# A windowed attention inside a one-core transformer kernel: values stationary in column halves, division on GpSimd, the sink as a 257th score column

## The chip, the cores and the metric

The kernel runs on one core of one Trainium2 chip. The metric is the device time of one execution in microseconds (us). Three runs of the kernel before took 963.71, 963.83 and 963.84 us; the median is 963.83 us.

## The reference, cut to what matters

The reference runs two blocks over 256 tokens of width 1024 in float32: first a block with an mLSTM layer, a feed-forward layer, a windowed attention and a second feed-forward layer, then a block with two more attentions. The change touches the windowed attention of the first block, called the first attention here:

```python
proj = h @ w_in                                   # 16 query heads, 4 key/value heads of 64
q, k = rope(q, positions), rope(k, positions)
scores = einsum('bcqhgd,bckhd->bchgqk', q, k_band) * (hd ** -0.5)
scores = where(mask, scores, -inf)                # |key - query| <= 128
m = maximum(max(scores, axis=-1), sink_l)
p = exp(scores - m[..., None])
denom = sum(p, axis=-1) + exp(sink_l - m)
out = einsum('bchgqk,bckhd->bcqhgd', p, v_band)
out = out / denom[..., None]
return out.reshape(B, S, Hq * hd) @ w_out         # then added to the residual
```

Each of the 16 query heads has a 256 x 256 score matrix, a sink logit that only enlarges the denominator, and a 256 x 64 output.

## The kernel before

Everything is written out by hand: each engine has one list of instructions (`block.sync`, `block.gpsimd`, the lists of TensorE, ScalarE and VectorE), and semaphores order them. No planner sets an order; what stands earlier in an engine's list runs earlier.

**Products.** Weights come from memory in 56 chunks of 1024 x 512 float32. SyncE loads each as two halves (`main`, L344) when `w_lo_ok` says that the half's old contents were split. ScalarE rounds a half to fp32r (`w_hi`, `split_half`, L1271, recorded at L1273) and VectorE subtracts to get the rest (`w_lo`, `rest_half`, L1806, at L1808). A product is then three matmuls (`mm3`, L450, lines 452 to 454). Activations that become stationary operands are split in the same way into a high and a low half: `to_stationary` (L510, transposes at L523) turns them on TensorE, `split_st` (ScalarE, L1249) writes the high half and counts `st_hi_ok`, `rest_st` (VectorE, L1745) the low half and counts `st_lo_ok`.

**The first attention.** Features of keys and queries lie on the partitions, 32 rows a head and half, so that four heads form a group. Four groups of four heads make the 16 heads, numbered n. The steps of one group j are:

- `a_queries` (L822): the query projection of a group, three matmuls of 256 columns each, 48 for all of it (24 for a half). VectorE rotates the result (`rotated`, L2120, lines 2125 to 2129) and counts `rot_ok`.
- `a_scores` (L837): 16 float32 matmuls, recorded as 32 instructions at L846; head g of the group works on rows 32g to 32g + 31 and writes to its own bank. It waits for `rot_ok` and, from the second group on, until VectorE has read the banks of the group before (`nm_ok`).
- `group_masked` (VectorE, L2186): for each head, two instructions (L2195, one for each half of the queries) scale, add the mask, write the scores `a_sm` to SBUF and take the maximum; after a drain L2199 compares it with the sink and negates it, counting `nm_ok`. After four heads L2202 adds the sinks for the extra term of the denominator.
- `a_exps` (ScalarE, L1494): two exponentials of 256 columns (L1501) with their sums, `p_ok`. It runs three heads ahead of the turns. After each group L1507 takes the exponentials of the sinks.
- `a_turn` (TensorE, L851): four transposes (L857) of the head's unnormalised weights into bank 5. ScalarE copies them to `a_pt` (L1515, two buffers) and counts `pt_ok`.
- `a_values` (TensorE, L861): four float32 matmuls, recorded as 8 instructions at L870. The turned weights are stationary, the 64 value columns move; tokens come out on the rows of bank 7. `o_ps` counts.
- `group_attended` (VectorE, L2205): sums and reciprocals of the group's denominators and one product of 128 x 512 (L2215) that divides the four heads and writes `a_o`, counting `o_ok`.

**The output projection.** `a_o` has tokens on its rows, so each of its 8 column tiles k is turned again: `a_out_turn` (L874), two transposes at L523, then `split_st` and `rest_st` into `y_hi` and `y_lo`. `a_out_tiles` (L881) multiplies tile k with the first half of the output weights: three matmuls of 512 columns for each of two row blocks. `mixer_rest` (L682) does the second half of the columns.

**The order around the change.** TensorE's list (from L887) begins with `a_scores(0)` and `a_queries(2)`. For each group it has: turn of the first head, values of the head before, scores of the next group, half of the last group's queries (j = 0 and 1), then for the three other heads a turn and the values of the head before. All output turns and output tiles stand in and behind the last group. Then come the 8 transposes of the meta tokens (L915), the last two tiles and `mixer_rest`. VectorE's list (from L2220) has, for each j: `group_attended(j - 1)`, `group_masked(j + 1)`, and for j = 0 and 1 a weight half and the rotation of queries 2 + j. ScalarE's list (from L1509) has, for each head n, the copy of turn n, the exponentials of n + 3, and after heads 0, 4 and 7 a weight half (`A_HALVES`, L125). GpSimd has nothing in this stretch: three loads are issued at L436 to L438, three more at L441 to L443 once the attention has been added to the residual (`h_ready` of 3).

## Time and profile before

| | |
|---|---|
| median of three runs | 963.83 us |
| span of the profiled execution | 963.6 us |
| TensorE busy (matmuls) | 939.2 us, 97% |
| VectorE busy | 585.4 us, 61% |
| ScalarE busy | 479.5 us, 50% |
| GpSimd busy | 24.7 us, 3% |
| granted TensorE clock over the span | 0.998 of 2.4 GHz |
| first attention, first scores to second half of its output projection | 348.46 to 405.37 us |

The profile is of one execution, and its span is its own time between the first and the last instruction; it lies 0.2 us below the median of the runs. The engines are named PE (TensorE), DVE (VectorE), ACT (ScalarE), POOL (GpSimd) and SP (SyncE). A TensorE instruction's end is modelled and overlaps its successors, so the distance between two starts says more of the queue than a duration. A float32 matmul appears as two instructions, an fp32r matmul and a transpose as one. Idle time of an engine counts only where another waits for it.

### The profile page before, as it was taken

The numbers are of one execution on the slowest core, as the hardware profiler recorded it, in microseconds if no ns is written. First come the engines' busy times: TensorE is split into PE (matmuls) and PEld (weight loads), VectorE is DVE, ScalarE is ACT, GpSimd is POOL, SyncE is SP. The second block draws the span as 40 slices with busy tenths as digits, with TensorE's granted clock in tenths as the row PEclk, the third lists the DMA queues.
The fourth block names the chain that finished last, engine by engine and source line by source line (L and its number), as shares of the span: only waits on it lengthen the run. The fifth ranks groups of instructions, "written<-read, shape, count | busy, mean of one in ns | idle before, by whom it ended". The sixth has DMA issues, their size and how long they took to land.

```text
span 963.6 us, 13667 instructions
## 1 busy us (share of the span) xinstructions
PE 939.2 (97%) x5035; PEld 779.7 (81%) x5035; DVE 585.4 (61%) x1078; ACT 479.5 (50%) x770; POOL 24.7 (3%) x39
## 2 busy tenths in 40 slices
PE   6999899999999999999999999999999999999996
PEld 6877678888888899878888888889987878878775
DVE  5866857655454678566463644877665556565665
ACT  6565556353443548454443434685344454445442
POOL 0014200000000000000000000000000000000000
PEclk9999999999999999999999999999999999999999
DMA  8542345545546322246546364232423242533441
GB/s 301 211 178 85 103 179 218 209 184 190 201 154 236 134 88 89 88 171 244 194 163 229 131 243 154 85 131 99 165 93 127 88 162 101 175 130 130 166 166 44
DMA packets 25607, 150.30 MB, mean 156 GB/s; under 512 B 3024, under 2 KB 3152, under 8 KB 11344
## 3 DMA queue, kind: packets, MB, share of 16 engines
q1 hardware_dynamic: 24912, 147.44, 41.9%
q0 software_dynamic: 640, 2.11, 0.7%
q8 instruction: 36, 0.59, 0.2%
q14 instruction: 19, 0.16, 0.0%
HBM read 148.50 MB, written 1.05 MB: 155 GB/s over the span
## 4 chain that ended last, share of the span: by engine, by line
PE 84%; DVE 7%; ACT 3%; DMA 3%; DVEq 1%; issue 1%; SPq 0%; ACTq 0%
PE bank L452 24%; PE bank L453 24%; PE bank L454 23%; DMA w_raw<-w_main_dram 3%; DVE w_lo L1808 2%; PE bank L523 1%; PE bank L1009 1%; PE bank L732 1%; DVE arena L2195 1%; PE bank L1024 1%; PE bank L1062 1%; PE bank L870 1%; PE bank L1044 1%; PE bank L1045 1%; PE bank L846 1%
## 5 line engine op out<-in xcount | busy, mean ns | idle before, releaser
L452 PE MATMUL bank<-w_hi,x_hi 128*128 128x512 f32 (+2 forms) x648 | 262.6, 405 | 1.7 <-DVE x_lo L1747 0.9
L453 PE MATMUL bank<-w_lo,x_hi 128*128 128x512 f32 (+2 forms) x648 | 253.9, 392 | 0.0
L454 PE MATMUL bank<-w_hi,x_lo 128*128 128x512 f32 (+2 forms) x648 | 252.2, 389 | 0.0
L452 PEld LDWEIGHTS bank<-w_hi,x_hi 128*128 128x128 f32 x648 | 122.2, 189 | 33.3 <-issue 5.6
L1722 DVE TENSOR_TENSOR w_lo<-w_raw,w_hi 128x2048 fp32r<-128x2048 f32 x50 | 114.4, 2292 | 57.0 <-ACT w_hi L1212 56.5
L454 PEld LDWEIGHTS bank<-w_hi,x_lo 128*128 128x128 f32 x648 | 121.7, 188 | 27.2
L453 PEld LDWEIGHTS bank<-w_lo,x_hi 128*128 128x128 f32 x648 | 122.0, 188 | 22.3
L1212 ACT ACTIVATE w_hi<-w_raw 128x2048 fp32r<-128x2048 f32 x54 | 103.2, 1917 | 58.1 <-DMA w_raw<-w_main_dram 52.0
L1808 DVE TENSOR_TENSOR w_lo<-w_raw,w_hi 128x2048 fp32r<-128x2048 f32 x51 | 116.2, 2283 | 4.8 <-ACT w_hi L1273 4.7
L1273 ACT ACTIVATE w_hi<-w_raw 128x2048 fp32r<-128x2048 f32 x50 | 94.9, 1907 | 14.7 <-DMA w_raw<-w_main_dram 14.2
L452 PE MATMUL bank<-x_hi,w_hi 128*128 128x256 f32 (+1 forms) x272 | 80.4, 296 | 8.9 <-DVE w_lo L1818 8.6
L1414 ACT ACTIVATE ffn_nat<-bank,stat 128x256 f32<-128x256 f32 x44 | 20.9, 474 | 136.9 <-PE bank L454 136.9
L2068 DVE SCALAR_TENSOR_TENSOR ffn_nat<-bank,stat,ffn_nat 128x256 f32<-128x256 f32 x44 | 21.1, 482 | 104.2 <-ACT ffn_nat L1414 104.1
L454 PE MATMUL bank<-x_hi,w_lo 128*128 128x256 f32 (+1 forms) x272 | 77.8, 286 | 0.0
L453 PE MATMUL bank<-x_lo,w_hi 128*128 128x256 f32 (+1 forms) x272 | 77.8, 286 | 0.0
L1490 ACT ACTIVATE arena<-arena,small 128x144 f32<-128x144 f32 x64 | 29.5, 461 | 76.4 <-DVE small L2172 76.4
L452 PE MATMUL bank<-s_hi,g_hi 128*128 128x512 f32 x166 | 65.4, 394 | 0.5 <-ACT arena L1233 0.4
L454 PE MATMUL bank<-s_hi,g_lo 128*128 128x512 f32 x166 | 65.4, 394 | 0.0
L453 PE MATMUL bank<-s_lo,g_hi 128*128 128x512 f32 x166 | 65.3, 393 | 0.0
L452 PEld LDWEIGHTS bank<-x_hi,w_hi 128*128 128x128 f32 x272 | 52.5, 193 | 12.4 <-issue 11.5
L452 PE MATMUL bank<-w_hi,s_hi 128*128 128x512 f32 x128 | 53.1, 415 | 0.7 <-DVE h L1999 0.4
L453 PEld LDWEIGHTS bank<-x_lo,w_hi 128*128 128x128 f32 x272 | 52.6, 193 | 0.0
(357 smaller groups left out, 1452.4 us busy)
## 6 DMA issues: line engine op xcount, KB each, us to landing
w_raw<-w_main_dram SPq DMA_DIRECT2D x111, 1024.0 KB, 4.9
s_raw<-w_side_dram SPq DMA_DIRECT2D x51, 512.0 KB, 4.2
w_raw<-w_main_dram SPq DMA_DIRECT2D x2, 512.0 KB, 6.7
h<-x_dram SPq DMA_DIRECT2D x2, 512.0 KB, 10.9
arena<-rows_dram POOLq DMA_DIRECT2D x2, 512.0 KB, 4.1
arena<-x_t_dram SPq DMA_DIRECT2D x1, 768.0 KB, 7.3
out_dram<-arena SPq DMA_DIRECT2D x1, 512.0 KB, 2.6
out_dram<-arena SPq DMA_DIRECT2D x2, 256.0 KB, 2.1
```

The lines of the kernel that those rows point to most:

```text
L452: pe.matmul(out, ah, bh, start=first, stop=False)
L453: pe.matmul(out, ah, bl, start=False, stop=False)
L454: return pe.matmul(out, al, bh, start=False, stop=last)
L523: ins = pe.transpose(b[:, M + r * P:M + (r + 1) * P], src(r, k), ident[:, :])
L732: ins = pe.transpose(bank[2][:, ks * S + r * P:ks * S + (r + 1) * P], ffn_nat[:, 1, r, ks * P:(ks + 1) * P], ident[:, :])
L1212: act.activation(w_hi[:, slot, 4 * g:4 * g + 4, :], w_raw[:, g, :, :], ACT.Copy).then_inc(w_hi_ok, 1)
L1273: act.activation(w_hi[:, slot, 4 * g:4 * g + 4, :], w_raw[:, g, :, :], ACT.Copy).then_inc(w_hi_ok, 1)
L1414: act.activation(ffn_nat[:, 0, r, :], acc[(n0 + r) % 2][:, 0:256], ACT.Silu, scale=stat[:, 24 + r:25 + r]).then_inc(silu_ok, 1)
L1490: ins = act.activation(tiles(r), tiles(r), ACT.Exp, bias=small[:, s0 + 2 + r:s0 + 3 + r], accum_out=small[:, s0 + 4 + r:s0 + 5 + r])
L1722: dve.tensor_tensor(w_lo[:, slot, 4 * g:4 * g + 4, :], w_raw[:, g, :, :], w_hi[:, slot, 4 * g:4 * g + 4, :], ALU.subtract).then_inc(w_lo_o ...
L1808: dve.tensor_tensor(w_lo[:, slot, 4 * g:4 * g + 4, :], w_raw[:, g, :, :], w_hi[:, slot, 4 * g:4 * g + 4, :], ALU.subtract).then_inc(w_lo_o ...
L2068: dve.scalar_tensor_tensor(out=ffn_nat[:, 1, r, :], in0=acc[b_][:, 256:512], scalar=root_col(r), in1=ffn_nat[:, 0, r, :], op0=ALU.mult, op ...
```

## The change

- The scores `a_sm` have rows of 258 with 257 in use. VectorE copies the sinks into column 256 for a whole group (`sinks`), and the exponentials run over 257 columns, so that their sum is the whole denominator. The extra steps for the sinks (L2202, L1507, `es_in`, `es_ok`) are gone.
- GpSimd takes, for each head, the sum to the power -1 (128 x 2) and multiplies the head's 128 x 2 x 256 weights with it in place; `a_turn` waits for its `pn_ok` instead of `p_ok`.
- `a_values(k)` works on a pair of heads: the 64 value columns are stationary, the turned weights of 256 tokens move, head 2k writes partitions 0 to 63 and head 2k + 1 partitions 64 to 127 of columns 0 to 255 of bank 7. That is already the feature-major tile k which the output projection needs: ScalarE (`a_out_high`) and VectorE (`a_out_low`) split it from there. `group_attended`, `a_o` and `a_out_turn` are gone.
- `a_pt` has four buffers, and the lists of all engines are put in a new order; output tiles stand from the third group on.

```diff
-A_HALVES = {0: (C_AOUT, 0), 4: (C_AOUT, 1), 7: (C_AOUT + 1, 0)}
+A_HALVES = {0: (C_AOUT, 0), 4: (C_AOUT, 1), 7: (C_AOUT + 1, 0), 13: (C_AOUT + 1, 1)}
...
-        a_sm, a_pt = (ar(4224, NG, R, S), ar(9344, NG, R, S)), ar(15744, 2, 4, P)
+        a_sm, a_pt = (ar(4160, NG, R, S + 2), ar(9344, NG, R, S + 2)), ar(6272, 4, 4, P)
...
+            pool.memset(recip, -1.0)
...
+            for n in range(NH):
+
+                st_, g = a_st[:, n // NG % 2, :, :], n % NG
+                t, root = a_sm[n // NG % 2][:, g, :, 0:S], st_[:, 3, g::NG]
+                pool.wait_ge(p_ok, n + 1)
+                pool.tensor_tensor(root, st_[:, 2, g::NG], recip.to_broadcast([P, R]), ALU.pow)
+                pool.drain()
+                pool.tensor_tensor(t, t, root.rearrange("p (r e) -> p r e", e=1).to_broadcast([P, R, S]), ALU.mult).then_inc(pn_ok, 1)
...
-                pe.wait_ge(p_ok, n + 1)
+                pe.wait_ge(pn_ok, n + 1)
...
+            def a_values(k):
+
+                pe.wait_ge(pt_ok, 2 * k + 2)
+                if k == 0:
                     pe.wait_ge(av_ok, 1)
...
+                else:
+                    pe.wait_ge(st_lo_ok, ST["a_out"] + k)
+                for kt in range(2):
+                    for n in (2 * k, 2 * k + 1):
+                        f, g = n % 2 * HD, n % NG
+                        ins = pe.matmul(bank[7][f:f + HD, 0:S], a_v[:, kt, g * HD:(g + 1) * HD],
+                                        a_pt[:, n % 4, 2 * kt:2 * kt + 2, :], start=(kt == 0), stop=(kt == 1))
+                ins.then_inc(tp_ready, 1)
...
                 a_turn(n)
-                if j:
-                    a_values(n - 1)
                 if j < NG - 1:
                     a_scores(j + 1)
+                if j:
+                    a_values(2 * j - 1)
                 if j < 2:
                     a_queries(3, j * KT // 2, (j + 1) * KT // 2)
...
+                else:
+                    a_out_tiles(4 * (j - 2))
+                a_turn(n + 1)
+                if j >= 2:
+                    a_out_tiles(4 * (j - 2) + 1)
+                a_turn(n + 2)
+                a_values(2 * j)
+                if j == 2:
+                    a_out_tiles(2)
+                elif j == 3:
+                    pe.wait_ge(um_ok, 1)
+                    pe.wait_ge(nm_ok, NH)
+                    for k in range(KT):
+                        ins = pe.transpose(bank[6][:, k * M:(k + 1) * M], um[0:M, k * P:(k + 1) * P], ident[0:M, 0:M])
+                    ins.then_inc(um_ps, 1)
+                a_turn(n + 3)
+                if j == 2:
+                    a_out_tiles(3)
             a_out_tiles(KT - 2)
+            a_values(KT - 1)
             a_out_tiles(KT - 1)
...
+            def a_out_high(k):
+
+                act.wait_ge(tp_ready, ST["a_out"] + k + 1)
+                act.activation(y_hi[:, k, :], bank[7][:, 0:S], ACT.Copy).then_inc(st_hi_ok, 1)
...
+                if n >= 4:
+                    act.wait_ge(tp_ready, ST["a_out"] + n // 2 - 1)
+                act.activation(a_pt[:, n % 4, :, :], bank[5][:, :].rearrange("p (a b) -> p a b", a=4), ACT.Copy).then_inc(pt_ok, 1)
                 if n + NG - 1 < NH:
                     a_exps(n + NG - 1)
+                if n >= 2 and n % 2 == 0:
+                    a_out_high(n // 2 - 1)
...
+            def a_out_low(k):
+
+                dve.wait_ge(st_hi_ok, ST["a_out"] + k + 1)
+                dve.tensor_tensor(y_lo[:, k, :], bank[7][:, 0:S], y_hi[:, k, :], ALU.subtract).then_inc(st_lo_ok, 1)
...
             for j in range(NG):
+                n = NG * (j + 1)
+                if j < NG - 1:
+                    sinks(j + 1)
+                    head_masked_a(n)
+                    head_masked_a(n + 1)
                 if j:
-                    group_attended(j - 1)
+                    a_out_low(2 * j - 1)
                 if j < NG - 1:
-                    group_masked(j + 1)
+                    head_masked_a(n + 2)
+                    head_masked_a(n + 3)
                 if j < 2:
                     rest_half(C_AOUT, C_AOUT % 2, j)
                     rotated(("aq", 2 + j), aqT[:, 2 + j, :, :])
...
+                a_out_low(2 * j)
+                if j >= 2:
+                    rest_half(C_AOUT + 1, (C_AOUT + 1) % 2, j - 2)
+            a_out_low(KT - 1)
```

`head_masked_a(n)` is the body of the old loop in `group_masked` for one head.

## Rows read from the trace of the kernel before

**Rows 1.** The page: header and busy time by engine.
```profile
span 963.6 us, 13667 instructions
...
PE 939.2 (97%) x5035; PEld 779.7 (81%) x5035; DVE 585.4 (61%) x1078; ACT 479.5 (50%) x770; POOL 24.7 (3%) x39
```

**Rows 2.** Windows 348.46 to 405.37 us: us, then busy time (instructions) of each engine, clock, DMA.
```profile
348.46:378.56 30.10, 29.54 (x293) 27.43 (x292) 25.34 (x82) 19.66 (x57) 0.00 (x0) 1.00 0.32 114
378.56:405.37 26.81, 26.50 (x196) 22.73 (x196) 15.74 (x45) 15.06 (x42) 0.00 (x0) 1.00 0.29 109
```

**Rows 3.** Timeline of TensorE: start us, us, engine, line, operation, names, shape, count.
```profile
356.13 0.60 PE L857 MATMUL bank<-ident,arena 128*128 128x128 f32 x4
356.93 2.01 PE L846 MATMUL bank<-arena 32*128 32x256 f32 x32 [0.20 <-DVE arena L2199]
...
363.18 0.63 PE L857 MATMUL bank<-ident,arena 128*128 128x128 f32 x4
363.65 1.00 PE L870 MATMUL bank<-arena 128*128 128x64 f32 x8
364.64 0.63 PE L857 MATMUL bank<-ident,arena 128*128 128x128 f32 x4
...
367.71 2.01 PE L846 MATMUL bank<-arena 32*128 32x256 f32 x32
...
378.56 2.01 PE L846 MATMUL bank<-arena 32*128 32x256 f32 x32 [0.24 <-DVE arena L2129]
...
400.94 0.60 PE L523 MATMUL bank<-ident,arena 128*128 128x128 f32 x4
401.47 0.66 PE L915 MATMUL bank<-ident,arena 16*128 16x16 f32 x8
```

**Rows 4.** Timeline of VectorE, 359 to 364 us, same columns.
```profile
359.78 0.23 DVE L2199 TENSOR_SCALAR arena<-arena,par 128x2 f32<-128x2 f32 x1
...
360.77 0.23 DVE L2199 TENSOR_SCALAR arena<-arena,par 128x2 f32<-128x2 f32 x1
...
363.14 2.28 DVE L1808 TENSOR_TENSOR w_lo<-w_raw,w_hi 128x2048 fp32r<-128x2048 f32 x1
```

**Rows 5.** The chain that ended last, in order of time: start us, us, what.
```profile
374.07 2.20 DVEq L2124
...
401.36 0.39 ACT s_hi L1249
401.77 0.44 DVE s_lo L1745
```

**Rows 6.** Timeline of TensorE, 728 to 731 us.
```profile
728.88 1.98 PE L1062 MATMUL bank<-arena 128*128 128x512 f32 x4 [0.33 <-ACT arena L1658]
```

**Rows 7.** Groups of instructions on GpSimd: line, form, count, busy us, mean ns, idle before.
```profile
L428 POOL TENSOR_TENSOR w_lo<-w_raw,w_hi 128x2048 fp32r<-128x2048 f32 x1 | 4.6, 4572 | 6.1 <-DVE w_lo L1808 6.1
L422 POOL TENSOR_TENSOR arena<-arena 128x128 f32<-128x128 f32 x8 | 3.5, 459 | 2.2 <-ACT arena L1347 2.2
```

**Rows 8.** Timelines of GpSimd and VectorE, 79 to 109 us.
```profile
81.55 1.53 POOL L433 TENSOR_SCALAR arena<-arena 128x512 f32<-128x512 f32 x1 [6.06 <-ACT arena L1338]
...
107.01 1.50 POOL L433 TENSOR_SCALAR arena<-arena 128x512 f32<-128x512 f32 x1
...
79.44 2.29 DVE L1808 TENSOR_TENSOR w_lo<-w_raw,w_hi 128x2048 fp32r<-128x2048 f32 x1 [1.79 <-ACT w_hi L1273]
...
107.76 0.17 DVE L1757 TENSOR_SCALAR stat<-stat 128x4 f32<-128x4 f32 x1 [0.98 <-ACT arena L1329]
108.00 0.53 DVE L1761 TENSOR_SCALAR stat<-stat 128x4 int32<-128x4 int32 x1
```

**Rows 9.** Timeline of ScalarE, 353 to 364 us.
```profile
353.87 0.51 ACT L1501 ACTIVATE arena<-arena 128x256 f32<-128x256 f32 x1 [12.12 <-DVE arena L2199]
...
354.77 0.19 ACT L1501 ACTIVATION_READ_ACCUMULATOR arena<-arena 128x1 f32 x1
...
363.92 0.58 ACT L1515 ACTIVATE arena<-bank 128x512 f32<-128x512 f32 x1
```

More of the change, by code:

```diff
@@ L319, in two_blocks @@
         c_bank = (bank[5], bank[7])
-        ang_ok, tab_ok, rot_ok, es_in, es_ok = (sem(n) for n in ("ang_ok", "tab_ok", "rot_ok", "es_in", "es_ok"))
+        ang_ok, tab_ok, rot_ok, pn_ok = (sem(n) for n in ("ang_ok", "tab_ok", "rot_ok", "pn_ok"))
         sc_ps, nm_ok, p_ok, pt_ps, pt_ok, ptm_ok, o_ps, o_ok = (
@@ L2205, in group_attended, with sinks @@
[L2205 to L2218 removed]
+            def sinks(j):
+                if j >= 2:
+                    dve.wait_ge(pt_ps, NG * (j - 1))
+                dve.tensor_copy(a_sm[j % 2][:, :, :, S:S + 1].rearrange("p g r e -> p g (r e)"),
+                                pcol("sink", NG * j, NG).rearrange("p (g r) -> p g r", r=1).to_broadcast([P, NG, R]))
@@ new lines, in head_masked_a @@
+            def head_masked_a(n):
+                j, g = n // NG, n % NG
+                st_ = a_st[:, j % 2, :, :]
+                dve.wait_ge(sc_ps, n + 1)
+                for r in range(R):
+                    dve.tensor_tensor_reduce(a_sm[j % 2][:, g, r, 0:S], as_bank[g][:, r * S:(r + 1) * S], a_mask[:, r, :], HD ** -0.5,
+                                             float(np.finfo(np.float32).min), ALU.add, ALU.max,
+                                             st_[:, 0, r * NG + g:r * NG + g + 1])
+                dve.drain()
+                dve.tensor_scalar(st_[:, 1, g::NG], st_[:, 0, g::NG], pcol("sink", n), -1.0, ALU.max, ALU.mult).then_inc(nm_ok, 1)
@@ L2220, in _ @@
+            def a_out_low(k):
+                dve.wait_ge(st_hi_ok, ST["a_out"] + k + 1)
+                dve.tensor_tensor(y_lo[:, k, :], bank[7][:, 0:S], y_hi[:, k, :], ALU.subtract).then_inc(st_lo_ok, 1)
             dve.wait_ge(c1_landed, 16)
-            group_masked(0)
+            sinks(0)
+            for n in range(NG):
+                head_masked_a(n)
             for j in range(NG):
+                n = NG * (j + 1)
+                if j < NG - 1:
+                    sinks(j + 1)
+                    head_masked_a(n)
+                    head_masked_a(n + 1)
```

97 lines of the change are left out of this document (10 added, 87 removed).

## The prediction

> **What bounds the kernel now.** I read the page first: TensorE is busy for 97% of the span [rows 1], so the first question is what TensorE has to do. Then its timeline around the change, from the first scores of the attention at 348.46 us to the second half of its output projection at 405.37. I cut it at the last of the four score blocks, 378.56, because something else is late on either side. Windows over the two stretches give 30.10 us with 29.54 busy and 26.81 us with 26.50 busy [rows 2]: TensorE hardly waits in either.
>
> In the first stretch it is nevertheless not alone. Score blocks start at 356.93, 367.71 and 378.56 [rows 3], 10.78 and 10.85 us apart. VectorE has a chain of nearly that length between two of them: the scores themselves, 2.01 us [rows 3], four heads at 0.99 each (359.78 to 360.77), then half a weight split and the rotation that the next scores need, from 363.14 to their start at 367.71 [rows 4]: 2.01 + 3.96 + 4.57 = 10.54. The chain that ended last runs over VectorE there [rows 5]. So work taken from TensorE in this stretch buys almost nothing: VectorE's loop is late next. In the second stretch VectorE is busy for 15.74 of 26.81 us and ScalarE for 15.06 [rows 2]; there TensorE's work is the time.
>
> **What the change takes from TensorE.** (a) The eight turns of the attention's output (`a_out_turn`, 16 transposes) go, all of them in the second stretch. Four transposes advance the queue by 0.53 us, 400.94 to 401.47 [rows 3], so eight pairs are 2.1, with the end of a batch in it; I take 1.9. (b) The values: now each head is 8 instructions in 0.99 us, 363.65 to 364.64, and a turn of a head is 0.47, 363.18 to 363.65 [rows 3]. Eight of the sixteen value blocks (heads 8 to 15) lie in the second stretch: 7.9 us. After the change there are eight blocks, one for each pair of heads, with 8 instructions of 256 columns; five of them come behind the last scores. No row has such a column half. From above: four fp32 instructions of 512 columns over the full height take 1.98 us [rows 6], so about 0.46 each with the last one's tail; 256 columns are half, 0.23, and eight one after the other 1.83, with 0.1 for a change of shape 1.92. From below: the scores, four heads on four row groups, put 32 instructions of the same 256 columns into 2.01 us [rows 3], eight in about 0.49; two heads side by side for two key tiles are then 0.97. I add 0.2 for entering and leaving the shape and take 1.17, because two halves that share no output partition are nearest to those row groups. Five blocks are 5.9 us, 2.0 less than now.
>
> The Trainium skill, TensorEngine Tiling (Array Packing), Key Properties, says that tiles load and multiply in parallel, and that a change of the tiling mode drains the engine; with its first half alone the five blocks would be 4.9 us and the kernel 1.0 faster than I forecast. The trace agrees with the first half for the row groups of the scores and shows nothing for column halves.
>
> **What it adds.** (c) GpSimd divides each head before its turn: a power of 128x2, a drain, a product of 128x512. Products of two tensors there cost 0.459 us at 128 columns and 4.572 at 2048 [rows 7], so 2.14 ns a column and 0.18 fixed: 1.28 for 512. From above, its operation of 512 columns with a scalar took 1.50 and 1.53 [rows 8]. I take 1.30, nearest to the line of its own kind. The power appears nowhere: from below it costs the fixed 0.18; from above I allow 2 us, above the whole 512-column operation, since each element may be worked out in software. I take 0.35 with the drain. That makes 1.65 a head, 26 us for sixteen, inside 57. As a throughput it fits; what counts is where a head comes fresh. The first does: its exponentials end at 354.96 [rows 9], VectorE's new copy of the sinks in front adds 0.2 and GpSimd 1.65, so the first turn starts near 356.85 instead of 356.13 and the second scores, right behind it, at 357.35 instead of 356.93: +0.4. Heads 1 to 3 are divided under the scores and queries. Head 4 is fresh again, and so is 8: its exponentials stand behind the copy of head 1 on ScalarE, copy 0.58, exponentials 1.09 [rows 9], GpSimd 1.65, and VectorE's weight split of 2.28 [rows 4] may hold the port before it. That turn waits up to 1.8 us, and all that TensorE has behind it. Its cover is VectorE's rotation, which the scores behind the turn need anyway; some 0.5 us of slack is left. Over 2.0 us a head the cover is gone and each excess is paid.
>
> (d) Turns 1 and 2 now stand with nothing between them, as do 3 and 4: transposes 0.60 [rows 3] and copy 0.58 [rows 9] less 0.47 make 0.8 us of waiting, for each of the first two groups, inside VectorE's loop and free by it. (e) ScalarE's new wait for a pair's values has the next copy and a weight half behind it; the one behind the second scores stands 2 us, while TensorE has 2.9 us of queries. Free. (f) VectorE loses the group divisions, which now lie under TensorE's scores (so nothing), and keeps eight subtractions of 0.44 [rows 5], one of them in the second loop: +0.3. The rotation's last additions read two SBUF tiles and can meet a GpSimd product, 0.3 in each loop; of TensorE's own delay now, 10.8 against 10.54, about as much goes. First stretch in sum: +0.4 + 0.3 - 0.1 = +0.6.
>
> (g) At the end the pair of heads 14 and 15 goes through TensorE, ScalarE 0.39 and VectorE 0.44 [rows 5] before the last output tiles, with nothing between: with 0.2 to fill and drain 1.05 us of waiting. (h) The sink as 257th column is one element per exponential, and four small exponentials go: nothing. (i) The meta-token transposes move, their work does not change. The last weight half is split on VectorE some 2 us later, near 399.8; the load that follows into its buffer is wanted on ScalarE from 407 us on, behind another half, and by TensorE only 11 us later. I cost it at nothing; were it late by those 2 us, ScalarE has room behind it. GpSimd's later loads wait for a point at 418 us, its heads end near 395. SyncE issues in the same order.
>
> **Sum.** Second stretch -1.9 - 2.0 + 1.05 = -2.9 us (rounded), first +0.6, together -2.3. The profiled execution spans 963.6 us [rows 1]; the median is 963.8, so 0.2 lies outside. 963.8 - 2.3 = 961.5 us.
>
> **Rivals.** *Slower, the port shared by VectorE and GpSimd.* The small 128x2 operation that ends each head on VectorE (L2199, `nm_ok`) could be held by a running GpSimd product. For it: the 128x4 operation from SBUF to SBUF at 108.00 took 0.53 us and ended with the GpSimd operation of 107.01. Against it: the like one at 107.76 took 0.17 beside the same operation [rows 8]. Held for 0.5 us at three heads of the first group and 0.9 us in all per loop, the second scores start 1.6 later and two loops are 1.8 longer: 3.4 dearer, 964.9. The sign turns once such waits in the first stretch pass 2.3 us.
>
> The Trainium skill, SBUF — State Buffer, Terms, calls the port pair an exclusive lock, held for the full instruction. One place of the trace agrees (108.00), one does not: the VectorE split of two inputs that ran to 81.73 while GpSimd began at 81.55 made that operation 1.53 instead of 1.50 [rows 8]. By the rule in full the port rival is the forecast.
>
> *The halves do not run side by side.* 1.92 a block instead of 1.17: five times 0.75 behind the last scores, 3.75, and 1.1 where value blocks stand in the loops: 966.3. *GpSimd is the bound.* At 2.6 us a head the turns of heads 3, 4, 8 and 13 to 15 wait for it, 5.5 us before the last scores and 2 behind: 7.6 dearer, 969.1; break-even with now near 2.1. *Better than forecast:* halves side by side with no cost of shape, GpSimd at 1.5: 960.2.
>
> **Chances.** Forecast 0.55 (its own range 960.2 to 963.6), the port 0.12, no overlap 0.12, GpSimd the bound 0.14, better 0.07. About 0.2%, 1.9 us, is what a measurement of this kernel can tell from no change. Of the forecast 0.38 is faster than that, 0.15 within, 0.02 slower; of the port case 0.05 is within. Together faster 0.45, same 0.20, slower 0.35. The range from 959.6 to 968.0 leaves out most of the GpSimd case (0.12) and 0.05 at the lower end.
>
> **What would show it.** Pair blocks of about 1.2 us (1.9: no overlap); 1.65 us from head to head on GpSimd where it runs on; score blocks still 10.7 to 11.1 apart, the last one 0.6 later; 24 us from there to the second projection half, against 26.81; 1 us of idle before the last output tiles; L2199 still at 0.23. I am wrong if the loops pass 12 us, if the power takes over 1 us, or if the second stretch stays near 26.

## The result and the profile after

The kernel after takes 965.47 us (median of 20 executions, 964.34 to 966.75), the one before 963.83 us (median of 20, 963.44 to 965.37): a ratio of 1.0014, 95% interval 1.0008 to 1.0021. The ratio is taken over all executions and lies nearer to that of the means, 965.44 and 964.01 us, than to that of the medians. By the medians the kernel is 1.6 us slower where 2.3 us faster was forecast; that lies within the 0.2% called no change and inside the range of 959.6 to 968.0.

Header and busy time from the page of the kernel after; they answer to [rows 1].

```profile
span 963.8 us, 13514 instructions
...
PE 933.2 (97%) x4955; PEld 768.2 (80%) x4955; DVE 581.7 (60%) x1066; ACT 478.3 (50%) x766; POOL 56.6 (6%) x72
```

TensorE has 6.0 us less to do, and the span is no shorter. Now the two stretches, cut at the same places as before: first scores to last scores, last scores to the second half of the projection. These windows answer to [rows 2]; columns as there.

```profile
347.58:381.49 33.91, 27.71 (x254) 22.48 (x253) 26.50 (x81) 19.70 (x58) 18.48 (x19) 0.95 0.29 102
381.49:405.44 23.95, 22.92 (x157) 16.26 (x157) 11.90 (x34) 15.03 (x38) 13.29 (x14) 1.00 0.28 105
```

The second stretch went from 26.81 to 23.95 us, 2.86 less; 2.9 was forecast. The first went from 30.10 to 33.91, 3.81 more; 0.6 was forecast. TensorE is busy 27.71 of those 33.91 us where it was busy 29.54 of 30.10, and the granted clock is 0.95 where it was 1.00. So the whole error of the sum sits in the first stretch. Its TensorE timeline (answers to [rows 3]; L868 is the turn of a head, L857 the scores, L882 the values of a pair):

```profile
356.55 0.65 PE L868 MATMUL bank<-ident,arena 128*128 128x128 f32 x4 [1.14 <-POOL arena L449]
357.13 2.01 PE L857 MATMUL bank<-arena 32*128 32x256 f32 x32
361.99 0.60 PE L868 MATMUL bank<-ident,arena 128*128 128x128 f32 x4
363.36 0.63 PE L868 MATMUL bank<-ident,arena 128*128 128x128 f32 x4 [0.78 <-ACT arena L1522]
363.92 1.08 PE L882 MATMUL bank<-arena 128*64 128x256 f32 x8
364.93 0.66 PE L868 MATMUL bank<-ident,arena 128*128 128x128 f32 x4
367.96 0.66 PE L868 MATMUL bank<-ident,arena 128*128 128x128 f32 x4 [2.37 <-POOL arena L449]
368.58 3.69 PE L857 MATMUL bank<-arena 32*128 32x256 f32 x32
```

Score blocks start 9.55, 11.45 and 12.91 us apart (before: 8.47, 10.78, 10.85). Three things are to be seen. The first turn waits 1.14 us for GpSimd. The turn of head 4 waits 2.37 us for it. And the score block behind that wait takes 3.69 us where its equal at 357.13 takes 2.01. Windows of one microsecond show why (the last three numbers are granted clock, DMA share and GB/s):

```profile
367.00:368.00 1.00, 0.04 (x1) 0.04 (x1) 0.91 (x2) 0.40 (x2) 1.00 (x2) 1.00 0.82 147
368.00:369.00 1.00, 1.00 (x8) 0.80 (x12) 0.94 (x4) 0.34 (x1) 0.86 (x2) 0.82 0.67 270
369.00:370.00 1.00, 1.00 (x13) 0.84 (x12) 0.00 (x0) 1.00 (x4) 1.00 (x2) 0.50 1.08 459
...
372.00:373.00 1.00, 1.00 (x12) 0.49 (x8) 0.71 (x4) 0.00 (x0) 0.86 (x2) 0.98 0.00 0
```

The clock falls to 0.50, the lower of its two levels (1.2 GHz), behind 2.4 us without work, and is back at 0.98 in the window from 372 us. (The 0.82 of the window from 368 us puts the fall at about 368.6, 0.7 us after TensorE had taken up work again.) Over 31 executions of this kernel (20 here, 11 in a later run) the mean granted clock of the span is 0.995 to 0.997; the kernel before has 0.997 to 0.999. So this is no accident of one trace. The Trainium skill, TensorE: Matmul & The Clock Gate, What's actually happening, says that the array's activity decides between the two levels; the trace agrees (0.50 behind the idle time).

GpSimd in the same stretch (L447 the power, L449 the product):

```profile
354.24 0.72 POOL L447 TENSOR_TENSOR arena<-arena,small 128x2 f32<-128x2 f32 x1 [219.83 <-ACT arena L1507]
355.45 1.04 POOL L449 TENSOR_TENSOR arena<-arena 128x512 f32<-128x512 f32 x1 [0.49 <-issue]
...
364.27 2.45 POOL L447 TENSOR_TENSOR arena<-arena,small 128x2 f32<-128x2 f32 x1 [2.28 <-ACT arena L1507]
366.87 1.04 POOL L449 TENSOR_TENSOR arena<-arena 128x512 f32<-128x512 f32 x1
```

VectorE in that time (answers to [rows 4]):

```profile
360.01 0.23 DVE L2208 TENSOR_SCALAR arena<-arena,par 128x2 f32<-128x2 f32 x1
...
360.50 0.42 DVE L2204 CUSTOM_DVE_ANT_0 arena<-bank,arena 128x256 f32<-128x256 f32 x1
361.00 1.02 DVE L2208 TENSOR_SCALAR arena<-arena,par 128x2 f32<-128x2 f32 x1
...
363.89 2.29 DVE L1813 TENSOR_TENSOR w_lo<-w_raw,w_hi 128x2048 fp32r<-128x2048 f32 x1
366.27 0.69 DVE L2130 TENSOR_TENSOR arena<-bank,arena 128x512 f32<-128x512 f32 x1
...
367.65 0.87 DVE L2134 TENSOR_TENSOR arena<-arena 128x256 f32<-128x256 f32 x2
```

A power takes 0.69 to 0.72 us, but the one of head 4 starts 0.4 us after the start of VectorE's weight split, ends 0.5 us after its end and takes 2.45. The other way round, the small operation that ends each head on VectorE (L2208; L2199 in [rows 4]) takes 0.23 us alone and 1.02 where a product of GpSimd was already running (360.95 to 361.99). Operations of VectorE that read a bank keep their length beside GpSimd (0.42 us, 0.69 us). The Trainium skill, SBUF — State Buffer, Who interferes with whom, states this pattern for VectorE: two SBUF inputs, or a scalar operation from SBUF to SBUF in one of the double-port modes, contend with GpSimd, whoever starts first keeps the ports for its whole instruction, and an operation with at most one SBUF input outside those modes doesn't contend. The trace agrees in these four cases (2.45 and 1.02 us held, 0.42 and 0.69 us not), but it does not show in which mode L2208 ran. The two places of [rows 8] where no such holding was seen (81.55 and 107.76 us) stay unexplained.

One premise of the sum was wrong as well, and did no harm. Every execution of either kernel for which both figures exist is 1.7 to 1.95 us above its span. So 1.8 us lie outside the span, not 0.2; by that the profiled execution of before, span 963.6, took about 965.4, which is the slowest of its 20 (965.37). The first scores of the attention start anywhere from 346.3 to 349.2 us in the traces of this study, with the same code ahead of them. The medians of the kernel before lie between 963.83 and 964.57 us, and the lengths of the two stretches are the sharper measure.

### The profile page after: what moved, and what is told of

Read it like the earlier page. It is cut to its first block, busy times and chain, and to the rows that moved or that the text cites. A ratio compares the mean times of both kernels' runs of the same rounds, so it can differ in the third digit from the quotient of the medians.

```text
span 963.8 us, 13514 instructions
## 1 busy us (share of the span) xinstructions
PE 933.2 (97%) x4955; PEld 768.2 (80%) x4955; DVE 581.7 (60%) x1066; ACT 478.3 (50%) x766; POOL 56.6 (6%) x72
## 3 DMA queue, kind: packets, MB, share of 16 engines
HBM read 148.50 MB, written 1.05 MB: 155 GB/s over the span
## 4 chain that ended last, share of the span: by engine, by line
PE 65%; issue 24%; DVE 5%; ACT 2%; POOL 1%; POOLq 1%; DMA 1%; DVEq 1%; SPq 0%; ACTq 0%
PE bank L463 18%; PE bank L464 18%; PE bank L465 18%; DVE w_lo L1813 1%; PE bank L534 1%; PE bank L1015 1%; POOL arena L449 1%; POOLq L448 1%; PE bank L1030 1%; PE bank L1068 1%; PE bank L1050 1%; PE bank L1051 1%; DMA w_raw<-w_main_dram 1%; PE bank L1049 1%; PE bank L882 1%
```

## The experiments

Every ratio is to the kernel before on the same chip. A row gives the distance between score blocks, the second stretch and the sum of both stretches, all three from one profiled execution, then the median and the ratio of all executions. The medians of before were 964.57 us beside e_fill, e_early, e_last and e_nodiv, 964.33 beside e_both, e_blast, e_same and e_nopow, 964.43 beside c_after, e_low, e_lowearly and e_lowhigh, and 964.30 beside e_um and e_nodivlast.

| run | loops of the first stretch | second | sum | median us | ratio (95%) |
|---|---|---|---|---|---|
| before | 8.47, 10.78, 10.85 | 26.81 | 56.91 | | |
| after | 9.55, 11.45, 12.91 | 23.95 | 57.86 | 965.47 | 1.0014 (1.0008 to 1.0021) |
| c_after | 9.55, 11.88, 12.48 | 23.95 | 57.86 | 965.05 | 1.0009 (1.0000 to 1.0018) |
| e_nodiv | 8.56, 10.52, 11.01 | 23.95 | 54.04 | 960.97 | 0.9967 (0.9954 to 0.9980) |
| e_nopow | 8.88, 10.80, 12.85 | 23.97 | 56.50 | 963.52 | 0.9987 (0.9978 to 0.9996) |
| e_fill | 9.55, 11.45, 11.91 | 25.64 | 58.55 | 964.86 | 1.0003 (0.9994 to 1.0012) |
| e_early | 9.55, 11.52, 12.12 | 23.93 | 57.12 | 965.23 | 1.0011 (1.0002 to 1.0020) |
| e_same | 9.53, 11.45, 12.55 | 28.24 | 61.77 | 969.25 | 1.0053 (1.0039 to 1.0067) |
| e_last | 9.55, 9.98, 11.40 | 24.37 | 55.30 | 962.17 | 0.9974 (0.9964 to 0.9985) |
| e_both | 9.56, 10.08, 10.62 | 25.34 | 55.60 | 963.32 | 0.9985 (0.9976 to 0.9994) |
| e_blast | 8.46, 10.57, 10.56 | 26.85 | 56.44 | 964.17 | 0.9998 (0.9989 to 1.0007) |
| e_low | 9.55, 10.01, 12.20 | 23.97 | 55.73 | 962.75 | 0.9988 (0.9979 to 0.9997) |
| e_lowearly | 9.55, 10.08, 11.57 | 24.09 | 55.29 | 963.26 | 0.9991 (0.9982 to 1.0000) |
| e_lowhigh | 9.55, 9.82, 12.54 | 23.96 | 55.87 | 964.74 | 1.0005 (0.9996 to 1.0014) |
| e_um | 9.56, 10.01, 11.39 | 24.34 | 55.30 | 962.81 | 0.9984 (0.9975 to 0.9993) |
| e_nodivlast | 8.56, 10.00, 11.00 | 23.96 | 53.52 | 960.85 | 0.9962 (0.9948 to 0.9975) |

**The kernel after again (c_after).** No edit.

> The kernel after, unchanged, on the chip of the next three. Theory (the first trace of before was of an execution at the slow end of its 20, so that nothing new lies outside the span): the time is again 1.7 to 1.9 us above the span in every execution, the score blocks start 9.55 and 11.45 us apart and the clock falls at the third, the time is 1.0 to 1.6 us above before. Rival (the loss lies outside the stretch, in the start of GpSimd or of the program): the stretch differs and the time outside the span does too.

The time outside the span is 1.75 to 1.83 us, the sum of the two stretches is 57.86 again, and the clock falls near the third scores. Counted from the first scores it fell some 0.8 us earlier this time, at about 368.2 us and before head 4's turn had even begun, so that the turn takes 1.11 us instead of 0.66. This lengthens the second loop and shortens the third. The second loop was expected at 11.45 and is 11.88; the median is 0.6 above before, where 1.0 at least was expected. The rival falls: neither the stretch nor the time outside the span differs.

```profile
368.34 1.11 PE L868 MATMUL bank<-ident,arena 128*128 128x128 f32 x4 [2.37 <-POOL arena L449]
```

**No division (e_nodiv).** It leaves out the division of the probabilities.

```diff
-                pe.wait_ge(pn_ok, n + 1)
+                pe.wait_ge(p_ok, n + 1)
...
-            for n in range(NH):
...
-                pool.tensor_tensor(root, st_[:, 2, g::NG], recip.to_broadcast([P, R]), ALU.pow)
-                pool.drain()
-                pool.tensor_tensor(t, t, root.rearrange("p (r e) -> p r e", e=1).to_broadcast([P, R, S]), ALU.mult).then_inc(pn_ok, 1)
```

> The division is left out: GpSimd does nothing for the heads and a head's turn waits for its exponentials. Theory (division costs the first turn 1.1 us and port waits of VectorE, and its share in the idle time that lowers the clock): the first loop is 1.1 us shorter, VectorE's small operation that ends a head stays at 0.23 us throughout, the third scores need no more than 2 us and start 10.5 us behind the second, 961 to 962. Rival (GpSimd's division is hidden and the loss is VectorE's order alone): loops of 11 us and more, 964 to 965.

The group of VectorE's small operations in this run, all sixteen (line, form, count, busy us, mean ns), and below it the one of the kernel after:

```profile
L2200 DVE TENSOR_SCALAR arena<-arena,par 128x2 f32<-128x2 f32 x16 | 3.7, 229 | 1.3
```

```profile
L2208 DVE TENSOR_SCALAR arena<-arena,par 128x2 f32<-128x2 f32 x16 | 5.3, 331 | 1.3
```

The first stretch is 30.09 us, that of before 30.10. So the division costs the first stretch all of its 3.8 us (0.99, 0.93 and 1.90 by loop), and everything else the change does there comes out even against before (+0.09, -0.26 and +0.16). The second stretch is 23.95 us with and without the division: there GpSimd is hidden.

**No power (e_nopow).** It leaves out the power and the drain, and multiplies by the plain sum.

```diff
-                pool.tensor_tensor(root, st_[:, 2, g::NG], recip.to_broadcast([P, R]), ALU.pow)
-                pool.drain()
-                pool.tensor_tensor(t, t, root.rearrange("p (r e) -> p r e", e=1).to_broadcast([P, R, S]), ALU.mult).then_inc(pn_ok, 1)
+                pool.tensor_tensor(t, t, st_[:, 2, g::NG].rearrange("p (r e) -> p r e", e=1).to_broadcast([P, R, S]), ALU.mult).then_inc(pn_ok, 1)
```

> GpSimd's power and drain are left out, it multiplies by the plain sum (so the heads are not divided but multiplied). Theory (the power's 0.83 us a head counts where a head comes fresh, and VectorE's split holds whatever GpSimd runs beside it): the first loop takes 8.8 us instead of 9.55, head 4's product is stretched to 2.4 us or more by the split, TensorE idles under 2 us there, the clock stays at 1.00, 962.5 to 963.5. Rival (the power was not what cost): 965 and more.

The first two loops lose 0.67 and 0.65 us, near the 0.83 from the start of a power to the start of its product. Head 4's product was held as expected, but for 1.98 us, not 2.4 or more. In the third the clock falls although no wait ahead of the scores passes 1 us, which the theory had not foreseen (the view ends within the score block, whose 32 instructions take 2.92 us):

```profile
367.50 0.63 PE L866 MATMUL bank<-ident,arena 128*128 128x128 f32 x4 [0.97 <-ACT arena L1520]
368.87 2.50 PE L855 MATMUL bank<-arena 32*128 32x256 f32 x28 [0.73 <-DVE arena L2132]
```

Here the clock fell behind waits of 0.78, 0.97 and 0.73 us and not behind a single long one. In its 11 executions the mean clock is 0.996 to 0.998: it seems not to fall in each.

**Idle time filled (e_fill).**

```diff
                 n = NG * j
+                if j == 1:
+                    pe.wait_ge(nm_ok, NG * 2)
+                    for i in range(16):
+                        pe.transpose(bank[6][:, i % 4 * P:(i % 4 + 1) * P], ident[:, :], ident[:, :])
                 a_turn(n)
```

> Sixteen transposes of the identity stand ahead of head 4's turn, where TensorE waits 2.37 us in the kernel after. Theory (the granted clock fell in the second loop because TensorE had stood idle): the third score block takes 1.94 us again instead of 3.62, the granted clock there is 1.00, head 4's turn starts as before within 0.3 us, and the kernel is 1.7 us faster than after, 963.8. Rival (the clock fell for something else, such as the kind of work around it or the moment): the block still takes 3.6 us and the time stays at 965.5.

```profile
365.05 1.91 PE L900 MATMUL bank<-ident 128*128 128x128 f32 x16
367.59 0.66 PE L868 MATMUL bank<-ident,arena 128*128 128x128 f32 x4 [0.63 <-POOL arena L449]
368.21 2.01 PE L857 MATMUL bank<-arena 32*128 32x256 f32 x32
...
379.51 0.66 PE L868 MATMUL bank<-ident,arena 128*128 128x128 f32 x4 [1.82 <-POOL arena L449]
380.12 3.69 PE L857 MATMUL bank<-arena 32*128 32x256 f32 x32
```

With the idle time filled the third scores take 2.01 us at full clock, and no wait ahead of them was changed but this one. One trace would not be enough, since the clock can fall in one execution and stay up in another (see e_lowearly below), but the mean clocks say the same: 0.998 in seven of these eleven executions, at most 0.997 in all 31 of the kernel after. Idle TensorE is what lowers the clock there. In the profiled execution it fell one loop later instead, behind the next wait for GpSimd, and cost the second stretch the same 1.7 us; there the theory's 963.8 failed. The median, 0.2 and 0.6 us below the two of the kernel after, can't be told from them.

The third loop of this trace, 11.91 us, is the one of the kernel after without a fallen clock. It is 1.0 us shorter, not 1.68, because VectorE's small operation now meets GpSimd's products at other moments: it is held for 0.85 us at one head (the row below) and 0.08 at another, where the kernel after loses 0.23.

```profile
372.16 1.08 DVE L2212 TENSOR_SCALAR arena<-arena,par 128x2 f32<-128x2 f32 x1
```

**Second turn early (e_early).**

```diff
                 if j < 2:
+                    a_turn(n + 1)
                     a_queries(3, j * KT // 2, (j + 1) * KT // 2)
                 else:
                     a_out_tiles(4 * (j - 2))
-                a_turn(n + 1)
+                    a_turn(n + 1)
```

> The turn of the second head of groups 0 and 1 stands ahead of the query tiles, so that head 4's and head 8's exponentials and divisions come 2 us earlier and no longer beside VectorE's weight split. Theory (GpSimd's division of head 4 and VectorE's loop of scores, masks, weight split and rotation end together, so VectorE's is late next): the third scores still start about 21 us after the first ones, TensorE stands idle 3 to 4 us ahead of them, the clock falls again, and the time is 965.5 within 0.7. Rival (GpSimd's power held behind the weight split is what delays the stretch): head 4's turn comes 3 us earlier and so do the third scores, no clock falls, 962 to 963.

```profile
365.92 0.63 PE L868 MATMUL bank<-ident,arena 128*128 128x128 f32 x4 [0.91 <-ACT arena L1523]
369.08 2.91 PE L857 MATMUL bank<-arena 32*128 32x256 f32 x32 [2.53 <-DVE arena L2135]
```

Head 4's turn comes 17.91 us behind the first scores instead of 20.38, and the third scores at 21.07 instead of 21.00: their wait is now VectorE's rotation. So GpSimd's late head was not alone. VectorE's loop ends at the same time, lengthened by its small operations, 1.02 and 0.30 us instead of 0.23 beside GpSimd's products. The clock falls all the same.

**Rotation ahead of the weight split (e_last).**

```diff
                 if j < 2:
-                    rest_half(C_AOUT, C_AOUT % 2, j)
                     rotated(("aq", 2 + j), aqT[:, 2 + j, :, :])
+                    rest_half(C_AOUT, C_AOUT % 2, j)
```

> VectorE rotates the next group's queries before it splits the weight half, in groups 0 and 1. Theory (VectorE's loop sets the stretch, and the split in it is what makes TensorE stand idle): the split goes under the scores, score blocks come 9.2 to 10 us apart instead of 11.45 and 12.91, the clock stays at 1.00, and the kernel takes 960.5 to 961.5. Rival (GpSimd's chain is the bound): the power of head 4 is held behind the rotation instead, blocks stay over 11 us apart, 964 to 965.

```profile
365.29 0.63 PE L868 MATMUL bank<-ident,arena 128*128 128x128 f32 x4 [0.97 <-ACT arena L1522]
365.84 2.01 PE L857 MATMUL bank<-arena 32*128 32x256 f32 x32
```

This version has the lowest median of those with the division in it and beats both kernels: 2.4 us less than before, ratio 0.9974 (0.9964 to 0.9985). The second loop has the length expected, the third is 1.4 us longer than its bound, and the median is 0.7 above the range given. Now the turn waits for ScalarE, which copies and exponentiates one head after the other.

**The same exchange in the kernel before (e_blast).** The same two lines of VectorE's order change places there.

> The same exchange of weight split and rotation on VectorE, made in the kernel before. Theory (there TensorE is busy 29.54 of the 30.10 us, so VectorE's order can give at most what TensorE is idle): 0.3 to 0.6 us faster than before, ratio 0.9994 or above. Rival (VectorE's loop alone set the first stretch, as the prediction had it, with TensorE's work hidden): its loop of 10.54 us loses 2.3 us, TensorE's 9.8 us of work a loop is next, 1.5 us faster, ratio 0.9985.

It gives 0.51 us in the loops (8.46, 10.57, 10.56) and 0.47 over both stretches, and nothing that the median could tell. This is the theory's side. VectorE's loop did bound the first stretch of before, but TensorE's work stood close behind it: the loops lose 0.2 and 0.3 us. The exchange pays only where the change has emptied TensorE, and the change pays only with the exchange.

**Both (e_both).** The diffs of e_last and e_early together.

> VectorE's rotation ahead of the weight split, and also the second turn of groups 0 and 1 ahead of the query tiles. Theory (with the split out of VectorE's loop, the loop is set by ScalarE's series of copy and exponentials from one turn to the next, which this lets start under the queries): the second and third loop take 9.6 to 10.6 us where the rotation moved alone has 9.98 and 11.40, the waits of 0.78 and 0.97 us ahead of turns go, 961.0 to 961.5. Rival (VectorE is still the bound): loops as with the rotation moved alone, 962.2.

The third loop is 10.62 as expected, the second does not gain, and at the fourth block of values a new wait stands (two of its eight instructions are shown):

```profile
381.47 0.44 PE L882 MATMUL bank<-arena 128*64 128x256 f32 x2 [1.32 <-DVE s_lo L2214]
```

The pair's residual stands behind the weight split on VectorE, so the 0.7 us won in the loops (20.70 for 21.38) go out again in the second stretch, which is 1.0 longer. The sum, 55.60, is no better than with the rotation moved alone, and the median of 963.32 is 1.8 us above the range expected.

**Halves on the same partitions (e_same).** Both heads of a pair write output partitions 0 to 63, one after the other; the odd head's values overwrite the even head's.

```diff
-                for kt in range(2):
-                    for n in (2 * k, 2 * k + 1):
-                        f, g = n % 2 * HD, n % NG
+                for n in (2 * k, 2 * k + 1):
+                    for kt in range(2):
+                        f, g = 0, n % NG
```

> Both heads of a pair write the same 64 output partitions, one after the other (the odd head's values land in the even head's place, so the output is another one). Theory (the two column halves really load and multiply side by side): a pair's eight instructions take 1.8 to 1.9 us instead of 1.01, the last stretch gets 4.2 us longer, 969.5 to 970.5. Rival (256 columns into 64 partitions are cheap by themselves): a pair still takes 1.0 to 1.1 us, 965.5.

```profile
362.80 1.94 PE L882 MATMUL bank<-arena 128*64 128x256 f32 x8
364.67 0.66 PE L868 MATMUL bank<-ident,arena 128*128 128x128 f32 x4
```

Eight instructions now advance the queue by 1.87 us instead of 1.01 (363.92 to 364.93 above), and the second stretch is 4.29 us longer: five blocks of 0.86. The 1.87 us lie close to the 1.83 that the prediction worked out for halves one after the other, so the two column halves do run side by side in the kernel after. The edit also brings each head's two key tiles behind each other, and no run separates that from the partitions. The median is 0.25 us below the range expected; the clock stayed at 1.00 in the windows behind this trace's third scores, where head 4's turn had waited 1.51 us instead of 2.37.

**Three attempts to do better (e_low, e_lowearly, e_lowhigh), and two runs to sort them out (e_um, e_nodivlast).** All five have the rotation first and move the meta-token transposes behind the last pair's values. e_low puts the pair's residual `a_out_low(2 * j)` ahead of the weight split, e_lowearly adds the early turn, e_lowhigh adds to e_low ScalarE's rounding of pairs 0 and 2 behind the next copy, e_um has the transposes alone, e_nodivlast has them and no division (the diff of e_nodiv).

All five, on TensorE:

```diff
-                elif j == 3:
-                    pe.wait_ge(um_ok, 1)
...
             a_values(KT - 1)
+            pe.wait_ge(um_ok, 1)
+            pe.wait_ge(nm_ok, NH)
+            for k in range(KT):
+                ins = pe.transpose(bank[6][:, k * M:(k + 1) * M], um[0:M, k * P:(k + 1) * P], ident[0:M, 0:M])
+            ins.then_inc(um_ps, 1)
             a_out_tiles(KT - 1)
```

e_low, e_lowearly and e_lowhigh, on VectorE (against e_last):

```diff
                 if j < 2:
                     rotated(("aq", 2 + j), aqT[:, 2 + j, :, :])
-                    rest_half(C_AOUT, C_AOUT % 2, j)
                 a_out_low(2 * j)
-                if j >= 2:
-                    rest_half(C_AOUT + 1, (C_AOUT + 1) % 2, j - 2)
+                rest_half(C_AOUT + j // 2, (C_AOUT + j // 2) % 2, j % 2)
```

e_lowhigh, on ScalarE:

```diff
+                if n in (3, 7):
+                    a_out_high(n // 2 - 1)
                 if n + NG - 1 < NH:
                     a_exps(n + NG - 1)
-                if n >= 2 and n % 2 == 0:
+                if n >= 4 and n % 2 == 0 and n != 6:
                     a_out_high(n // 2 - 1)
```

> The rotation ahead, then the residual of the pair, then the weight split on VectorE; and the meta-token transposes moved behind the last pair's values. Theory (what is left in the stretch is two waits of 0.32 and 0.35 us for the residual that stood behind the split, and 0.94 us of idle time before the last output tiles that the 0.66 us of transposes can fill): against the rotation moved alone 0.3 to 0.7 us less in the loops and 0.6 us less at the end, 961.0 to 961.5, 3 us faster than before. Rival (the meta-token part becomes late for the tiles that need it): the second half of the projection starts no earlier, 962.

> The same with the second turn of groups 0 and 1 ahead of the query tiles. Theory (the early turn keeps ScalarE from setting the second loop, and what it lost before was the residual's wait behind the split, 1.32 us at the fourth values block): first stretch 29.6 to 30.2 us, 960.5 to 961.3. Rival (an early turn delays the queries and with them the rotation in each loop): first stretch 30.3 or more, 961.5 to 962.5.

> As the one with rotation, residual and meta-token transposes moved, and ScalarE's rounding of two pairs behind the next copy instead of ahead of it. Theory (ScalarE's series of copies and exponentials is what heads 4 and 8 wait for, 0.97 us each): each of these two waits is 0.26 us shorter, 0.5 us less than without it. Rival (those turns wait for GpSimd's product as well, which lands at the same time): no change.

> The rotation ahead of the split (as in the run that moved it alone), and the meta-token transposes behind the last pair's values. Theory (port waits of VectorE depend on how its small operations fall against GpSimd's, and VectorE's order in the loops is untouched here): loops of 9.55, 9.98 and 11.40 us again, 0.35 us of idle time before the last output tiles instead of 0.94, 961.5 to 962.0 and 2.5 to 3 us faster than before. Rival (the loop of 12.20 us came from the transposes moved behind the last values): a third loop of 12 us here too.

> The same, with the division left out. Theory (GpSimd's division and the port cost the stretch 1 us in the first loop and what VectorE's small operations are held, 1 to 2 us, in the others): loops of 8.5, 9.6 and 10.2 us, no small VectorE operation over 0.25 us, 959.0 to 960.0. Rival (the turns' series on ScalarE sets the second and third loop with or without a division): 8.5, 10.0 and 11.4 us, 960.7.

e_low, VectorE's rotation and the first 20 of the 32 score instructions behind it:

```profile
378.33 1.62 DVE L2133 TENSOR_TENSOR arena<-arena 128x256 f32<-128x256 f32 x2
```

```profile
380.00 1.36 PE L857 MATMUL bank<-arena 32*128 32x256 f32 x20 [1.12 <-DVE arena L2133]
```

None of the three beat e_last, and all three missed their expected times: e_low by 1.3 us, e_lowearly by 2.0 with a first stretch of 31.20 instead of 30.2 at most, e_lowhigh by being 2.0 us slower than e_low instead of 0.5 faster. e_um's median of 962.81 is 0.8 above the range it was given. In e_low the two additions of the rotation take 1.62 us where they take 0.87 in the kernel after, and the fourth scores wait 1.12 us for them. e_um, with VectorE's order as in e_last, has 10.01 and 11.39 us again, so it was the order on VectorE that brought 12.20, not the transposes. Our reading, not shown by a run of its own: small operations that move by a third of a microsecond meet GpSimd's otherwise, and a whole loop moves with them. e_lowhigh took 0.19 us off each of its two waits (0.97 to 0.78) where 0.26 was expected, and its fourth scores wait 1.64 us for the rotation. In the tail the wait ahead of the last output tiles is 0.35 us instead of 0.94, as expected, but the turn of head 15 now waits 0.23 and the transposes stand in the gap: 24.34 against 24.37 us, no gain. The medians also differ where the sums agree: e_lowearly has 55.29 and 963.26, e_last 55.30 and 962.17. The clock is one reason that shows. It is 0.996 to 0.998 in e_lowearly's executions and 0.997 to 0.999 in those of e_last; of e_lowhigh's eleven, seven lie at 0.994 to 0.996. The waits alone don't decide whether it falls. TensorE's waits ahead of the third scores are the same in e_both and e_lowearly (0.91 and then 1.09 us); at the scores the clock stayed up in the first trace and fell in the second:

```profile
367.52 2.01 PE L857 MATMUL bank<-arena 32*128 32x256 f32 x32 [1.09 <-DVE arena L2135]
```

```profile
366.08 2.91 PE L857 MATMUL bank<-arena 32*128 32x256 f32 x32 [1.09 <-DVE arena L2134]
```

One execution of e_lowearly, left out of its ratio and of the median in the table, took 1862.97 us, 1861.2 of them inside its span at full clock; there is no trace of it and its cause is open.

e_nodivlast decides what sets the loops once the rotation goes first. The rival was right for the second loop, 10.00 us without a division and 10.01 with it, and nearer for the third, 11.00 without and 11.39 with it. Its waits are those of e_last:

```profile
373.86 0.63 PE L860 MATMUL bank<-ident,arena 128*128 128x128 f32 x4 [0.78 <-ACT arena L1513]
...
377.06 0.63 PE L860 MATMUL bank<-ident,arena 128*128 128x128 f32 x4 [0.97 <-ACT arena L1513]
```

So the division costs 1.0 us in the first loop and 0.4 in the other two in this order, against 3.8 in the order of the kernel after.

## Why the prediction was wrong

**The bound of each stretch: right, by a small margin.** VectorE's loop and TensorE's work were named for the first stretch, TensorE alone for the second. The unchanged 23.95 us of e_nodiv bear out the second. For the first, e_blast shows VectorE's loop ahead of TensorE's own work by only 0.2 to 0.3 us a loop in the kernel before.

**(a), (b), (g), the second stretch: -2.86 for -2.9, in part by luck.** By distances between starts in the two traces, the eight value blocks of before took 7.19 us there, not 7.9, and the five pairs take 5.13, not 5.9. Both were put 0.7 to 0.8 too high, so their difference is -2.06 where -2.0 was forecast. The 16 transposes of the output took 1.53 us for the 1.9 taken, and the tail waited 0.94 us for 1.05. What the forecast left out (turns, meta-token transposes and output tiles in their new order) sums to -0.2. The prediction had read its prices from places where the next instruction starts late; in the second stretch of before it starts sooner, 0.14 us after the first of two transposes and 0.82 after the start of a value block:

```profile
392.71 0.39 PE L523 MATMUL bank<-ident,arena 128*128 128x128 f32 x2
392.85 0.48 PE L452 MATMUL bank<-w_hi,s_hi 128*128 128x512 f32 x1
...
396.37 1.00 PE L870 MATMUL bank<-arena 128*128 128x64 f32 x8
397.19 0.48 PE L452 MATMUL bank<-w_hi,s_hi 128*128 128x512 f32 x1
```

The rival of halves one after the other is excluded by the pair's 1.01 us.

**(c), GpSimd: the step that failed first, 0.99 us in the first loop.** The product was taken at 1.30 us and advances the queue by 1.00; the power with its drain was taken at 0.35 and takes 0.83. A head takes 1.83 us (357.29 to 359.12 us on GpSimd) for 1.65, and the very first one 2.25 (354.24 to 356.49). The first loop lost 1.08 us where +0.4 was forecast, 0.99 of them by e_nodiv. The term mis-sized is the power, for which no row existed; the value taken lay near its lower bound.

**(f) and the port rival: the step that failed most, 0.9 us in each of the other two loops.** The forecast gave 0.3 us a loop to the rotation's additions and nothing to the small operation that ends a head. The additions lost 0.11 us. In the second loop the small operation lost 0.79 at 361.00; together that is 0.90 of the 0.93 us that the loop is longer than in e_nodiv, and e_early shows that head 4's earlier turn doesn't shorten it. In the third loop, where the clock stays up (e_fill), the division costs 0.90 again: 11.91 against 11.01 us. That is the rival's mechanism and its "0.9 us in all per loop", given a chance of 0.12. Its other 1.6 us, at the heads of the first group, did not come: the 0.53 lost at 355.75 ended before head 0's turn could start. So its 964.9 lies near the measured 965.47 in part by luck. The rival was argued down from one small operation of 0.17 us beside GpSimd [rows 8]. The rule of the Trainium skill in SBUF — State Buffer, Terms, which the text set aside there, was the better guide: the trace agrees with 1.02 us for 0.23.

**(c), head 4, and the clock: a term put at nothing, 1.0 us in the third loop.** The text saw that VectorE's split "may hold the port before it" and that the turn would wait up to 1.8 us under VectorE's rotation. It waits 2.37, and the rotation, which ends at 368.52 where the scores start at 368.58, does cover it. But the cover was priced at nothing, and it was idle time on TensorE. The clock fell behind it, and the scores at the lower level cost 1.68 us (3.69 less 2.01), of which the third loop keeps 1.0 (12.91 against 11.91 in e_fill). The forecast had no term for the clock, although it takes TensorE's time in a stretch that VectorE holds open. Waits under a cover are free only as long as the engine's clock stays up.

**(d), (e), (h), (i): no cost seen.** The waits of turns 2 and 6 are 0.78 us and free inside VectorE's loop. Without division the first stretch is 30.09 us against 30.10, so sinks, wider exponentials and the pair's subtractions cost nothing there together. The last weight half is split at 399.94 us, as foretold (399.8). The 0.78 us became part of a bound only in e_last.

**The sum.** Measured by stretch: +3.81 - 2.86 = +0.95 us. The division makes up 3.82 of the first: 0.99 GpSimd's time for the first head, 0.93 and 0.90 VectorE's operations held beside GpSimd, 1.0 the clock (the last two told apart by e_fill's one trace). The medians say +1.6 and +0.6 and the ratios +1.3 and +0.9 in two comparisons, whose intervals both hold 0.95.

Of the three signs given for being wrong, one came in full (the third loop passed 12 us). The power stayed under 1 us where it ran free and took 2.45 behind the split. The second stretch came out at 24 as foretold.

## What to carry to other kernels

Where work is taken off TensorE in a stretch that another engine holds open, ask what the holding engine has in that loop that could stand elsewhere, before counting anything saved: here one exchange of two steps turned +0.95 us into -1.6 by the stretches. Count the idle time that is left as a price, since TensorE's granted clock may fall behind it. And work moved to GpSimd is to be laid beside every VectorE operation that has both inputs, or its one input and its output, in SBUF: each side held the other here (0.23 us became 1.02, 0.69 became 2.45).

## What was not expected of the hardware

- A power of 128x2 elements on GpSimd takes 0.69 us, two thirds of a product of 128x512 (1.04 us). The first power of the stretch was followed by its product only 1.21 us after its own start, all others that ran free by 0.83.
- TensorE's clock fell to its lower level behind 2.37 us of waiting and also behind waits of 0.78, 0.97 and 0.73 us (e_nopow); with waits of 0.78, 0.97 and 0.45 in the same places it stayed up (e_nodiv). With the same waits of 0.91 and 1.09 us it stayed up in one trace (e_both) and fell in another (e_lowearly).
- Two heads' values, 8 instructions of 256 columns, take 1.01 us on two column halves of one bank and 1.87 on the same partitions.
- A device time is 1.7 to 1.95 us above its span in every execution here, so a span is not to be set against a median.
